# A decoder layer in fp32: the statistics of two layer norms taken with tokens on partitions

## What is computed

```python
h = layer_norm(alpha * h + 0.5 * swiglu(h, ffn1...), ln1_g, ln1_b)
h = layer_norm(alpha * h + hybrid_mixer(h, ...), ln2_g, ln2_b)
h = layer_norm(alpha * h + 0.5 * swiglu(h, ffn2...), ln3_g, ln3_b)
return h[:, N_META:]

def layer_norm(x, g, b):
    mu = mean(x, axis=-1); var = mean(square(x - mu), axis=-1)
    return (x - mu) * rsqrt(var + 1e-5) * g + b
```

## Time and profile before

| | |
|---|---|
| median of 3 runs | 1013.48 us (1012.99 to 1014.37) |
| the profiled execution | 1013.6 us, span 1011.9 us |
| TensorE matmul busy | 992.6 us, 98% of the span |
| VectorE busy | 718.1 us, 71% |
| ScalarE busy | 500.2 us, 49% |
| GpSimd busy | 120.5 us, 12% |
| mean granted TensorE clock | 0.996 |

### The profile page before, as it was taken

The page is one execution under the profiler, slowest core; times in us unless marked ns, Lnnn a source line. Parts: engine busy times, 40 slices in busy tenths (PEclk is TensorE's granted clock), DMA queues, the critical chain, the costliest instruction groups (busy, mean ns, idle before and its releaser), DMA issues.

```text
span 1011.9 us, 19045 instructions
## 1 busy us (share of the span) xinstructions
PE 992.6 (98%) x7048; PEld 911.2 (90%) x7048; DVE 718.1 (71%) x1299; ACT 500.2 (49%) x883; POOL 120.5 (12%) x96
## 2 busy tenths in 40 slices
PE   8999999999999999999999999999999999999996
PEld 8999999999999989699866778889999999988885
DVE  6988888888223263599998633699989989932336
ACT  6655655566221254546336732566656665812121
POOL 0000000000211253044221205310000000000000
PEclk9999999999999999999999999999999999999998
DMA  7223232323222323131210102113323233333212
GB/s 253 85 88 121 87 120 83 124 70 115 87 86 87 106 75 107 43 123 50 80 42 1 43 1 84 42 42 126 124 83 124 93 114 105 126 96 106 93 57 84
DMA packets 30847, 90.47 MB, mean 89 GB/s; under 512 B 4688, under 2 KB 5328, under 8 KB 30800
## 3 DMA queue, kind: packets, MB, share of 16 engines
q1 hardware_dynamic: 30800, 89.83, 27.0%
HBM read 87.72 MB, written 2.10 MB: 89 GB/s over the span
## 4 chain that ended last, share of the span: by engine, by line
PE 80%; DVE 15%; ACT 2%; issue 1%; DMA 1%; SPq 0%; DVEq 0%; ACTq 0%
PE ps L1253 38%; PE ps L1311 22%; PE ps L1176 9%; DVE sc L2244 3%; DVE top L2243 3%; PE ps L1448 1%; PE ps L1716 1%; PE ps L1730 1%; DVE qk L2283 1%; PE ps L1756 1%; DVE wlo L1920 1%; PE ps L1513 1%; PE ps L1361 1%; PE ps L1359 1%; DMA wraw<-in_ffn_w_up 1%
## 5 line engine op out<-in xcount | busy, mean ns | idle before, releaser
L1253 PE MATMUL ps<-tsum,whi 128*128 128x264 f32 (+1 forms) x1280 | 243.1, 282 | 0.5 <-ACT ht L813 0.5
L1253 PEld LDWEIGHTS ps<-tsum,whi 128*128 128x128 f32 x1280 | 202.3, 188 | 0.7 <-issue 0.7
L1253 PE MATMUL ps<-tsum,wlo 128*128 128x264 f32 (+1 forms) x640 | 180.3, 282 | 0.0
L1253 PE MATMUL ps<-xh,whi 128*128 128x264 f32 (+1 forms) x480 | 135.4, 282 | 0.3 <-ACT sil L813 0.3
L1253 PE MATMUL ps<-xl,whi 128*128 128x264 f32 (+1 forms) x480 | 135.5, 282 | 0.0
L752 ACT ACTIVATE whi<-wraw 128x1408 fp32r<-128x1408 f32 (+1 forms) x48 | 74.7, 1556 | 122.9 <-PE ps L1311 121.8
L1253 PE MATMUL ps<-xh,wlo 128*128 128x264 f32 (+1 forms) x480 | 135.3, 282 | 0.0
L1830 DVE TENSOR_TENSOR wlo<-wraw,whi 128x1408 fp32r<-128x1408 f32 (+1 forms) x38 | 70.1, 1845 | 85.9 <-ACT whi L752 85.9
L1311 PE MATMUL ps<-hh,whi 128*128 128x264 f32 (+1 forms) x462 | 124.2, 323 | 0.0
L1311 PE MATMUL ps<-hh,wlo 128*128 128x264 f32 (+1 forms) x462 | 123.5, 322 | 0.0
L1311 PE MATMUL ps<-hl,whi 128*128 128x264 f32 (+1 forms) x462 | 123.3, 321 | 0.0
(11 more groups left out here) (304 smaller groups left out, 1854.2 us busy)
## 6 DMA issues: line engine op xcount, KB each, us to landing
wraw<-in_ffn_w_gate SPq DMA_DIRECT2D x43, 512.0 KB, 4.2
wraw<-in_ffn_w_up SPq DMA_DIRECT2D x42, 512.0 KB, 4.4
wraw<-in_ffn_w_down SPq DMA_DIRECT2D x32, 384.0 KB, 3.2
wraw<-in_ffn_w_down SPq DMA_DIRECT2D x32, 320.0 KB, 3.5
wraw<-in_w_in SPq DMA_DIRECT2D x19, 512.0 KB, 4.4
wraw<-in_w_out SPq DMA_DIRECT2D x8, 512.0 KB, 4.4
out<-zrow SPq DMA_DIRECT2D x8, 256.0 KB, 2.0
x<-in_x SPq DMA_DIRECT2D x3, 528.0 KB, 7.5
```

The costliest lines, as they stand in the source:

```text
L1253: mm = pe.matmul(ps[:, bank, 0:(HT, HALF_SEQ)[p // 2]], w[:, k * P:(k + 1) * P], v[:, k, :], start=(first and k == 0 and n == 0), stop=(k ...
```

## The change

The sums over features now come out with tokens on partitions. In `stats` the data (a slice of `zsum`, of `ssum`, of the last tile or of its square) is the stationary operand and one column of `mean_w` the moving one, so the result is one column with a token on each partition: three tiles of 88 tokens for each half of p = 0, two of 128 for p = 1. Copy, square, variance, root and reciprocal then run on [88 x 3] or [128 x 2]. The new `spread_stat` brings the mean, and later the reciprocal deviation, back to all partitions: the column is broadcast as stationary operand and multiplied by the identity. `finish_stats` sets TensorE's order at the end of each norm. In the first product of p = 0 two spreads are put after kk = 10 and kk = 17. VectorE's order changes, and `early` becomes 2 for p = 1.

```diff
+        stat = sb("stat", [P, 2, 16])
+        stat_spread = sem("stat_spread")
+        def stat_tiles(p, e):
+            R = (HT // 3, P)[p]
+            t0 = e * HT if p == 0 else N_META + e * HALF_SEQ
+            return [(i, R, slice(t0 + i * R, t0 + (i + 1) * R)) for i in range(3 - p)]
+        def token_sums(p, e, v):
+            return ps[0:(HT // 3, P)[p], 4 + 2 * v + e, 320:320 + 3 - p]
+        def token_stat(p, e, v):
+            return stat[0:(HT // 3, P)[p], e, 4 * v:4 * v + 3 - p]
...
                     act.wait_ge(s["stats_done"], 2 * e + 1)
-                    act.activation(part(sil[:, 0, :], p, e), part_bank(4, p, e), ACT.Square).then_inc(s["mu2_done"], 1)
+                    act.activation(token_stat(p, e, 0), token_sums(p, e, 0), ACT.Copy).then_inc(s["mu2_done"], 1)
+                    act.activation(token_stat(p, e, 1), token_sums(p, e, 0), ACT.Square).then_inc(s["mu2_done"], 1)
                     act.wait_ge(s["varc_done"], e + 1)
-                    act.activation(part(sil[:, 1, :], p, e), part_bank(6, p, e), ACT.Sqrt).then_inc(s["sd_done"], 1)
+                    act.activation(token_stat(p, e, 3), token_stat(p, e, 2), ACT.Sqrt).then_inc(s["sd_done"], 1)
...
                         if (e, kk) == (1, 7):
                             stats(0, 0)
+                        if (e, kk) == (1, 10):
+                            spread_stat(0, 0, 0)
+                        if (e, kk) == (1, 17):
+                            spread_stat(0, 0, 1)
...
                 pe.wait_ge(s["sums_done"], KT + 1)
-                for b, v in ((4, zsum), (6, ssum)):
-                    pe.matmul(part_bank(b, p, e), mean_w[:, :], part(v, p, e), start=True, stop=False)
-                    done, last = ("z_done", x[:, KT - 1, :]) if b == 4 else ("sq_done", sil[:, 1, :])
+                for v, (w, done, last) in enumerate(((zsum, "z_done", x[:, KT - 1, :]), (ssum, "sq_done", sil[:, 1, :]))):
                     pe.wait_ge(s[done], KT + e)
-                    pe.matmul(part_bank(b, p, e), mean_w[:, :], part(last, p, e), start=False, stop=True)\
-                        .then_inc(s["stats_done"], 1)
+                    for i, R, tokens in stat_tiles(p, e):
+                        dst = token_sums(p, e, v)[:, i:i + 1]
+                        pe.matmul(dst, w[:, tokens], mean_w[:, 0:1], start=True, stop=False)
+                        mm = pe.matmul(dst, last[:, tokens], mean_w[:, 0:1], start=False, stop=True)
+                    mm.then_inc(s["stats_done"], 1)
+
+            def spread_stat(p, e, v):
+                if v == 0:
+                    pe.wait_ge(F[p]["mu2_done"], 2 * e + 2)
+                else:
+                    pe.wait_ge(F[p]["rstd_done"], e + 1)
+                for i, R, _ in stat_tiles(p, e):
+                    mm = pe.matmul(ps[:, 4 + 2 * v + e, i * R:(i + 1) * R],
+                                   token_stat(p, e, 2 * v)[:, i:i + 1].broadcast_to([R, P]), ident[0:R, 0:R],
+                                   start=True, stop=True)
+                mm.then_inc(stat_spread, 1)
+
+            def finish_stats(p):
+                if p == 1:
+                    spread_stat(p, 0, 0)
+                stats(p, 1)
+                if p == 1:
+                    spread_stat(p, 0, 1)
+                keep_warm(3)
+                spread_stat(p, 1, 0)
+                keep_warm(5)
+                spread_stat(p, 1, 1)
+                keep_warm(WARM_NORM - 12)
...
             ffn(0)
-            stats(0, 1)
-            keep_warm(WARM_NORM)
+            finish_stats(0)
             mixer()
-            stats(1, 1)
-            keep_warm(WARM_NORM)
+            finish_stats(1)
...
                 def half_centres(e, ks):
+                    dve.wait_ge(stat_spread, 4 * p + 2 * e + 1)
...
                 def half_scales(e):
-                    dve.wait_ge(s["rstd_done"], e + 1)
+                    dve.wait_ge(stat_spread, 4 * p + 2 * e + 2)
...
-                early = 3 if p == 0 else 1
+                early = 3 if p == 0 else 2
                 last_residual(0)
-                variance(0)
-                half_centres(0, range(early))
                 if p == 1:
                     last_residual(1)
+                variance(0)
                 inverse(0)
-                half_scales(0)
+                half_centres(0, range(early))
                 if p == 0:
+                    half_scales(0)
                     last_residual(1)
                 variance(1)
-                half_centres(1, range(min(early, 2)))
                 inverse(1)
-                half_centres(1, range(2, early))
+                if p == 1:
+                    half_scales(0)
+                half_centres(1, range(early))
                 half_scales(1)
```

More of the change, by code:

```diff
@@ L2132, in variance @@
                 def variance(e):
-                    var = part_bank(6, p, e)
+                    var = token_stat(p, e, 2)
                     dve.wait_ge(s["stats_done"], 2 * e + 2)
-                    dve.wait_ge(s["mu2_done"], e + 1)
-                    dve.tensor_tensor(var, var, part(sil[:, 0, :], p, e), ALU.subtract).then_inc(s["var_done"], 1)
+                    dve.wait_ge(s["mu2_done"], 2 * e + 2)
+                    dve.tensor_tensor(var, token_sums(p, e, 1), token_stat(p, e, 1), ALU.subtract).then_inc(s["var_done"], 1)
                     dve.wait_ge(s["var_done"], e + 1)
@@ L2141, in inverse @@
                     dve.wait_ge(s["sd_done"], e + 1)
-                    dve.reciprocal(part_bank(6, p, e), part(sil[:, 1, :], p, e)).then_inc(s["rstd_done"], 1)
+                    dve.reciprocal(token_stat(p, e, 2), token_stat(p, e, 3)).then_inc(s["rstd_done"], 1)
                 def centre(z, mean):
```

## The result

| | before | after |
|---|---|---|
| median | 1012.99 us (5 runs, 1012.50 to 1014.37) | 1018.94 us (5 runs, 1015.66 to 1019.93) |
| profiled execution, span | 1011.9 us | 1018.2 us |
| mean granted TensorE clock | 0.996 | 0.993 |

The ratio is 1.005 (95% interval 1.0039 to 1.006): slower, by 6.0 us, and outside the range given. The runs after the change spread over 4.3 us, and the longer ones have the lower mean granted clock: 1019.93 at 0.993, 1019.22 at 0.994, 1018.94 at 0.993, 1016.82 at 0.995, 1015.66 at 0.997. That was the first hint.

What follows compares the result with a forecast made beforehand. TensorE led 80% of the chain, so norms were taken to matter only from the last product's end to the second `xh` tile. +1.10 - 0.45 = +0.65 on 1013.6 gave 1014.25, median forecast 1014.2, range 1012.0 to 1016.0.

Steps and rivals of the forecast that it cites:

- The clock: Rival: one-column products lower TensorE's clock in the 5 us after each product, about 4 us per norm: 1020, chance 0.04.
- From there on each stage follows the last: After the second norm's `xh` tiles: TensorE's and ScalarE's steps are equally long, so both norms' shifts reach the end.
- First norm, +1.10 predicted: First norm (p = 0): scaling 0.22 earlier after the product's end, which itself comes 1.32 later; the whole +1.10 us.
- The price of a pair: One weight load and one-column matmul in the statistics or spreads: 0.075 us with 88-column weights, 0.108 with 128, set by the load.
- The two spreads: Inside the first norm's product, after kk = 10 and kk = 17: six pairs each at 0.108, new unhidden work, +1.30 us.
- P': End of the first norm's last product after the change, predicted at P + 1.32 us.
- P: End of a norm's last product: 366.05 in the first norm before the change, 645.25 in the second.
- Second norm, -0.45 predicted: Second norm (p = 1): scaling 0.11 earlier and `xh` of tile 1 at 652.9 against 653.36, -0.45 us.
- no idle time at either spread inside the product: First norm, after kk = 10 and kk = 17: no wait expected in front of the spreads.
- TensorE's queue, not the reciprocal, limits the scaling: Behind the first norm's statistics: TensorE's queue with warm calls is what is late next, putting scaling at P'+5.84.
- the delay isn't absorbed by the mixer: Against the rival that the first norm's delay is absorbed later, leaving only -0.45: 1013.0, chance 0.08.
- GpSimd holds back a larger gain in the first norm: First norm: GpSimd's six `xl` tiles run without a break, so a gain above some 0.5 us would be held back.

Runs made afterwards that it cites:

- e1_wide: Changed kernel with 64 equal columns of `mean_w` instead of one in every statistics product: 1015.55 us, ratio 1.0024 to the kernel before.
- b_stat: Kernel before with only the new tile `stat` declared and unused: 1014.19 us against 1012.74, ratio 1.0014.
- e6_fewwarm: Changed kernel with 64-column statistics products, small values in `sil`, no `stat`, and 0, 2, 7 warm calls for 3, 5, 8: 1011.71 us, ratio 0.9989.
- e8_hybrid: `e6_fewwarm` with the halves e = 0 of both norms done as in the kernel before: 1011.54 us, ratio 0.9989 to the kernel before.
- e9_best: `e6_fewwarm` with only half e = 0 of the first norm as before, and GpSimd's `sel`, `selp` masks moved behind its `xl` tiles: 1011.48 us, ratio 0.9988.
- b_thin20: Kernel before with one column instead of 128 in all 20 warm calls behind each norm's statistics: 1015.37 us, ratio 1.002.
- e4_thinwarm: Kernel before with one column instead of 128 in the first 8 of 20 warm calls behind each norm's statistics: 1012.86 us, ratio 1.0001.

## Why the prediction was wrong

The forecast was 1014.2 in a range of 1012.0 to 1016.0, with 0.14 on slower. The clean part of it, without a low clock, can be read from `e1_wide`: 1015.55 against 1012.94. That lies inside the range, but it would have been luck: +2.6 is four times the +0.65 that was added up, because of the terms of points 2 to 4. The rest is the clock.

1. **The clock, the step that failed.** It stood among the rivals with 0.04: "If one-column products let the clock drop in the 5 us of TensorE's order after each product". That is what happened, in both norms of the profiled execution. What was set against it was "the 64-column pairs ran at a granted clock of 1.00". Those rows show a stream of 64 columns; `e1_wide` shows that 64 columns are what makes the difference, so the row chosen as nearest in price was no evidence for the clock. The price was off as well: about 4 us a norm was put on the whole 5 us, while the stretch covered less of it, and the norms lost 18.71 - 17.19 = 1.5 and 13.17 - 11.53 = 1.6. Together that is 3.2 of the 6.0 us. Nor did the rival's own sum come out: 1014.2 and two times 4 are 1022, not 1020.
2. **"From there on each stage follows the last": a term that was missing.** The mixer did follow, to 0.02 us. The rest did not: it took 1.2 us more, as it does with the 128 bytes of `stat` alone (`b_stat`). The prediction priced the instructions of the change and never its declaration.
3. **First norm, +1.10 predicted, 17.19 - 15.71 = +1.48 measured with a full clock.** The price of a pair was right: 24 pairs of 88 columns in 1.82 (359.86 to 361.68), 0.076 each. The two spreads were not 1.30. Six pairs took 0.59, less than the 0.65 predicted, but the ordinary product behind them took 0.21 (363.45 to 363.66) where 0.12 is usual, and so it was behind `stats(0, 0)` (361.68 to 361.89) and behind the second spread. With these three places P' is P+1.52 and not P+1.32. Behind the residual TensorE began 0.77 after P', not 0.68: the data are now the weights, so each pair's load stands behind the wait too (argued, since no run separates it). The statistics ended at P'+2.65 for P'+2.48, and scaling came at P'+6.03 for P'+5.84.
4. **Second norm, -0.45 predicted, 11.53 - 11.77 = -0.24 measured with a full clock.** Scaling at P+5.95 for a predicted P+5.76; the pairs took 0.111 ((651.55 - 649.77) / 16), as priced. The steps of `xh` from tile 0 to tile 1 were 1.43, as predicted, down from 1.79.
5. **Right:** thin pairs cost what the width of their weights says, 0.076 for 88 columns and 0.111 for 128, for a predicted 0.075 and 0.108, and 64 moving columns cost the same as one; no idle time at either spread inside the product; TensorE's queue, not the reciprocal, limits the scaling (`e6_fewwarm` took 2.4 us out of it); the delay isn't absorbed by the mixer; and GpSimd holds back a larger gain in the first norm, shown by the 0.55 in `e8_hybrid`, whose first norm had gained 1.0 against the kernel before.

The sum as the runs give it: +1.48 - 0.24 + 1.23 = +2.5, and with the two low stretches, 1.5 and 1.6, +5.6, for a measured +6.0; the 0.4 left over is less than the stretch before the first norm varies by. The forecast of +0.65 missed 1.2 by the address, 0.6 by small terms, all on one side, and 3.2 by the clock.

`e6_fewwarm`, `e8_hybrid` and `e9_best` beat the kernel before by 0.11 to 0.12%, a little over 1 us, with intervals that end just under 1: the statistics with tokens on partitions pay, if only just, when their products are 64 columns wide, the small values are put where nothing moves, and most warm calls between the spreads go.

## What to carry to other kernels

Where each matmul has its own weights, one with a single column was no cheaper here than one with 64 (24 pairs in 1.88 and 1.90), but the low stretches came only with single columns. So try columns that are not needed before filling waits with warm calls. A row that is near in price is not for that reason near in everything: ask of each reference row whether it shares the property that the rival turns on. And allocate new small tiles in free parts of old ones, or measure the kernel once with the tile alone.

## What the runs showed that was not expected

- Forty one-column pairs, back to back, were followed by a granted clock of 0.50, in both norms (`b_thin20`). Sixteen did nothing (`e4_thinwarm`).
- The same kernel falls in some executions and not in others: 1015.66 at a mean clock of 0.997 and 1019.93 at 0.993 with the same code.
- 128 unused bytes in each partition moved a loop of 1680 matmuls from 198.89 to 200.34 us, another from 204.54 to 204.80, and the first down products the other way by 0.2 (`b_stat`).
- An ordinary product behind a run of fp32 pairs took 0.21 for 0.12 (363.45 to 363.66 after the change).
- An operation of VectorE on [88 x 3] took 0.88 for 0.16 beside a memset of GpSimd (`e9_best`), and 0.43 beside a shorter one (`e8_hybrid`).
